# Activation halves moved 64 bytes apart in SBUF under a three-product float32r matmul kernel

## What is computed

```python
def conv_ffn(h, w_in, conv_w, conv_b, w_out):
    a = dwconv3(h @ w_in, conv_w, conv_b)
    gate, up = jnp.split(a, 2, axis=-1)
    return (jax.nn.silu(gate) * up) @ w_out
...
def _sq_relu_mlp(hn, w1, w2):
    a = jax.nn.relu(hn @ w1)
    return (a * a) @ w2
```

## Time and profile before

| | |
|---|---|
| time, median of 3 runs | 2044.6 us (2042.35 to 2045.34) |
| the profiled execution, its time | 2041.65 us |
| its span, first to last instruction | 2039.9 us |
| mean granted TensorE clock | 0.983 of full speed |
| TensorE matmul busy | 1938.5 us, 95% |
| weight load busy | 1709.0 us, 84% |
| DVE, ACT, POOL busy | 1251.0, 920.6, 217.7 us |

### The profile page before, as it was taken

The page is one execution under the profiler, slowest core; times in us unless marked ns, Lnnn a source line. Parts: engine busy times, 40 slices in busy tenths (PEclk is TensorE's granted clock), DMA queues, the critical chain, the costliest instruction groups (busy, mean ns, idle before and its releaser), DMA issues.

```text
span 2039.9 us, 33160 instructions
## 1 busy us (share of the span) xinstructions
PE 1938.5 (95%) x13225; PEld 1709.0 (84%) x13225; DVE 1251.0 (61%) x1853; ACT 920.6 (45%) x1438; POOL 217.7 (11%) x171
## 2 busy tenths in 40 slices
PE   4999989999999899999979998999999999989998
PEld 3776647778887479999979997998899999879997
DVE  6355466543654556678577767656975567787564
ACT  4344344322332242158465554347554444565353
POOL 2100104430542000011000000000010010000001
PEclk8999989999999899999999999999999999999999
DMA  8611464433222523223435544532444544224553
GB/s 357 229 69 63 164 228 165 167 125 111 83 90 85 206 83 128 101 83 104 145 136 170 208 162 142 174 137 83 139 171 167 177 174 145 94 94 170 186 182 124
DMA packets 43950, 296.78 MB, mean 145 GB/s; under 512 B 4976, under 2 KB 6128, under 8 KB 11696
## 3 DMA queue, kind: packets, MB, share of 16 engines
q1 hardware_dynamic: 36576, 247.48, 35.0%
q10 hardware_dynamic: 6048, 42.50, 5.9%
q0 software_dynamic: 1200, 5.02, 0.7%
HBM read 293.94 MB, written 1.05 MB: 145 GB/s over the span
## 4 chain that ended last, share of the span: by engine, by line
PE 83%; DVE 8%; ACT 4%; DMA 3%; issue 1%; POOL 1%; SPq 0%; ACTq 0%; DVEq 0%; POOLq 0%
PE acc L456 23%; PE acc L457 22%; PE acc L458 22%; DVE w_lo L393 2%; PE acc L451 2%; PE wk L550 2%; PE acc L453 2%; PE acc L452 2%; PE wk L1672 1%; DMA ada_first<-in_w_ada 1%; DMA ada_ring<-in_w_ada 1%; ACT w_hi L383 1%; PE wk L730 1%; PE acc L1661 1%; PE wk L1401 1%
## 5 line engine op out<-in xcount | busy, mean ns | idle before, releaser
L456 PE MATMUL acc<-Hhi,w_hi 128*128 128x272 f32 (+2 forms) x2304 | 740.5, 321 | 29.4 <-DVE Hlo L772 10.1
L457 PE MATMUL acc<-Hlo,w_hi 128*128 128x272 f32 (+2 forms) x2304 | 717.9, 312 | 0.0
L458 PE MATMUL acc<-Hhi,w_lo 128*128 128x272 f32 (+2 forms) x2304 | 717.5, 311 | 0.0
L393 DVE TENSOR_TENSOR w_lo<-w_raw,w_hi 128x1024 fp32r<-128x1024 f32 (+2 forms) x472 | 575.5, 1258 | 183.9 <-ACT w_hi L383 182.4
L383 ACT ACTIVATE w_hi<-w_raw 128x1024 fp32r<-128x1024 f32 (+2 forms) x472 | 452.3, 1005 | 432.9 <-PE acc L458 339.6
L456 PEld LDWEIGHTS acc<-Hhi,w_hi 128*128 128x128 f32 x2304 | 437.1, 190 | 79.7 <-issue 42.0
L457 PEld LDWEIGHTS acc<-Hlo,w_hi 128*128 128x128 f32 x2304 | 437.4, 190 | 22.1
L458 PEld LDWEIGHTS acc<-Hhi,w_lo 128*128 128x128 f32 x2304 | 436.5, 189 | 23.0
L456 PE MATMUL acc<-Fhi,w_hi 128*128 128x256 f32 (+2 forms) x864 | 265.1, 307 | 2.8 <-DVE w_lo L393 1.5
L458 PE MATMUL acc<-Fhi,w_lo 128*128 128x256 f32 (+2 forms) x864 | 264.6, 306 | 0.0
L457 PE MATMUL acc<-Flo,w_hi 128*128 128x256 f32 (+2 forms) x864 | 264.3, 306 | 0.0
(11 more groups left out here) (393 smaller groups left out, 2426.6 us busy)
## 6 DMA issues: line engine op xcount, KB each, us to landing
w_raw<-in_w_ffn_in SPq DMA_DIRECT2D x44, 1024.0 KB, 4.9
ada_ring<-in_w_ada ACTq DMA_DIRECT2D x40, 1024.0 KB, 4.9
w_raw<-in_w_mlp_in SPq DMA_DIRECT2D x32, 1024.0 KB, 4.9
w_raw<-in_w_mlp_out SPq DMA_DIRECT2D x32, 1024.0 KB, 4.9
w_raw<-in_w_ffn_out SPq DMA_DIRECT2D x32, 704.0 KB, 4.1
ada_first<-in_w_ada SPq DMA_DIRECT2D x8, 1024.0 KB, 18.4
w_raw<-in_w_ret_v SPq DMA_DIRECT2D x8, 1024.0 KB, 4.9
w_raw<-in_w_ret_g SPq DMA_DIRECT2D x8, 1024.0 KB, 4.8
```

Of the source, the lines that this page charges most:

```text
L393: dve.tensor_tensor(w_lo[:, r, a:b], w_raw[:, r, a:b], w_hi[:, r, a:b].bitcast(F32), ALU.subtract).then_inc(lo_done, 1)
L456: pe.matmul(o, w_hi[:, r, w], x_hi(k), start=k == 0, stop=False)
L457: pe.matmul(o, w_hi[:, r, w], x_lo(k), start=False, stop=False)
L458: mm = pe.matmul(o, w_lo[:, r, w], x_hi(k), start=False, stop=k == last)
```

## The change

The program keeps every instruction and their order on every engine; operands move. `A` goes from 64 to 128 modulo 256 (64 bytes further). The pairs, in bytes modulo 256, high half and low half:

| pair | before | after |
|---|---|---|
| H 512 (hyb, ffn0_in) | 192, 192 | 128, 192 |
| H 512 as read by ret_k, ret_q, ret_v, ret_g, now called R | 192, 192 | 192, 128 |
| H 256 (ffn1_in) | 192, 192 | 192, 128 |
| H 272 (ab, mlp0_in, c, mlp1_in) | 128, 128, then 64 more for each chunk | unchanged |
| F 512 (ffn0_out) | 64, 64 | 128, 192 |
| F 256 (ffn1_out) | 64, 64 | 192, 128 |
| F 272 (mlp0_out, mlp1_out) | 64, 64, then 64 more for each chunk | 128, 192; rows of 288 columns, then 128 more for each chunk |
| AT and SG (hyb_out) | 64, 64 | 128, 128 |
| rv_out (ret_out) | 64, 64 | 192, 192 |
| AB (ab_out0) | 64, 64, then 64 more for each chunk | 128, 128, then 64 more |

The remaining edits move work buffers by 64 bytes so that nothing overlaps. The diff, cut to its core:

```diff
-        A = (at_const[0] + 127) // 128 * 128 + 64
-
-        H_hi = {T1: at("Hhi512", [P, DC, T1], h0 + 64, F32R), SEQ: at("Hhi256", [P, 16, SEQ], h0 + 64, F32R),
+        A = (at_const[0] + 255) // 256 * 256
+
+        H_hi = {T1: at("Hhi512", [P, DC, T1], h0, F32R), SEQ: at("Hhi256", [P, DC, SEQ], h0 + 64, F32R),
                 T2: at("Hhi272", [P, 16, T2], h0, F32R)}
-        H_lo = {T1: at("Hlo512", [P, DC, T1], h0 + HB + 64, F32R), SEQ: at("Hlo256", [P, 16, SEQ], h0 + HB + 64, F32R),
+        H_lo = {T1: at("Hlo512", [P, DC, T1], h0 + HB + 256 + 64, F32R), SEQ: at("Hlo256", [P, DC, SEQ], h0 + HB + 256 + 0, F32R),
                 T2: at("Hlo272", [P, 16, T2], h0 + HB, F32R)}
+
+        R_hi, R_lo = at("Rhi", [P, DC, T1], h0 + 64, F32R), at("Rlo", [P, DC, T1], h0 + HB + 256 + 0, F32R)
...
-        F_hi = {T1: at("Fhi512", [P, FFH, T1], A + 16 * KB, F32R), SEQ: at("Fhi256", [P, FFH, SEQ], A + 16 * KB, F32R),
-                T2: at("Fhi272", [P, MLH, T2], A + 16 * KB, F32R)}
-        F_lo = {T1: at("Flo512", [P, FFH, T1], A + 38 * KB, F32R), SEQ: at("Flo256", [P, FFH, SEQ], A + 38 * KB, F32R),
-                T2: at("Flo272", [P, MLH, T2], A + 38 * KB, F32R)}
+        F_hi = {T1: at("Fhi512", [P, FFH, T1], A + 16 * KB, F32R), SEQ: at("Fhi256", [P, FFH, SEQ], A + 16 * KB + 64, F32R),
+                T2: at("Fhi272", [P, MLH, 288], A + 16 * KB + 0, F32R)}
+        F_lo = {T1: at("Flo512", [P, FFH, T1], A + 38 * KB + 64, F32R), SEQ: at("Flo256", [P, FFH, SEQ], A + 38 * KB + 0, F32R),
+                T2: at("Flo272", [P, MLH, 288], A + 38 * KB + 64, F32R)}
...
-        rv_out = at("rv_out", [P, 4, 2048], A + 16 * KB, F32R)
+        rv_out = at("rv_out", [P, 4, 2048], A + 16 * KB + 64, F32R)
...
-            ret = (lambda k: H_hi[T1][:, k, LAT:T1], lambda k: H_lo[T1][:, k, LAT:T1])
-            project(pe, "ret_k", *hyb, need=h_need(pe, 2))
+            both = (lambda k: R_hi[:, k, :], lambda k: R_lo[:, k, :])
+            ret = (lambda k: R_hi[:, k, LAT:T1], lambda k: R_lo[:, k, LAT:T1])
+            project(pe, "ret_k", *both, need=h_need(pe, 2))
```

More of the change, by code:

```diff
@@ L231, in stack_kernel @@
         ada_ring = at("ada_ring", [P, 2, SLOT], nt0 + 18 * KB)
-        ada_rows = [at("ada_rows0", [P, 2, 256], A + 32 * KB), at("ada_rows1", [P, 1, 256], h0 + 16 * KB + 64)]
+        ada_rows = [at("ada_rows0", [P, 2, 256], A + 32 * KB), at("ada_rows1", [P, 1, 256], h0 + 16 * KB + 128)]
         sq2 = at("sq2", [P, 2, T2], A + 85 * KB)
@@ L239, in stack_kernel @@
         last = at("last", [P, DC, SEQ], h0)
-        F_hi = {T1: at("Fhi512", [P, FFH, T1], A + 16 * KB, F32R), SEQ: at("Fhi256", [P, FFH, SEQ], A + 16 * KB, F32R),
-                T2: at("Fhi272", [P, MLH, T2], A + 16 * KB, F32R)}
-        F_lo = {T1: at("Flo512", [P, FFH, T1], A + 38 * KB, F32R), SEQ: at("Flo256", [P, FFH, SEQ], A + 38 * KB, F32R),
-                T2: at("Flo272", [P, MLH, T2], A + 38 * KB, F32R)}
[L245 to L248, removed]
+        F_hi = {T1: at("Fhi512", [P, FFH, T1], A + 16 * KB, F32R), SEQ: at("Fhi256", [P, FFH, SEQ], A + 16 * KB + 64, F32R),
+                T2: at("Fhi272", [P, MLH, 288], A + 16 * KB + 0, F32R)}
+        F_lo = {T1: at("Flo512", [P, FFH, T1], A + 38 * KB + 64, F32R), SEQ: at("Flo256", [P, FFH, SEQ], A + 38 * KB + 0, F32R),
+                T2: at("Flo272", [P, MLH, 288], A + 38 * KB + 64, F32R)}
+        cgu = at("cgu", [P, 2, 2, T1], A + 60 * KB + 64)
+        sg = at("sg", [P, 2, T1], A + 68 * KB + 64)
+        hid = at("hid", [P, 2, T1], A + 72 * KB + 64)
+        hid2 = at("hid2", [P, 2, 2, T2], A + 72 * KB + 64)
         g_sb = at("g_sb", [P, 4, T1], A + 16 * KB)
@@ L266, in stack_kernel @@
         ro = at("ro", [P, 8, 2, SEQ], A)
-        rv = at("rv", [P, 4, 2048], A + 16 * KB)
-        rv_out = at("rv_out", [P, 4, 2048], A + 16 * KB, F32R)
[L269 to L277, removed]
+        rv = at("rv", [P, 4, 2048], A + 16 * KB + 64)
+        rv_out = at("rv_out", [P, 4, 2048], A + 16 * KB + 64, F32R)
+        r_ctx = at("r_ctx", [P, 2, SEQ], A + 88 * KB + 64)
+        rq = at("rq", [P, 8, SEQ], A + 48 * KB + 64)
+        rg = at("rg", [P, 16, SEQ], A + 56 * KB + 64)
+        r_dist = at("r_dist", [P, 2, 2, SEQ], A + 72 * KB + 64)
+        r_dec = [at(f"r_dec{i}", [P, 4, SEQ], A + (76 + 4 * i) * KB + 64) for i in range(2)]
+        r_rope = at("r_rope", [P, 2, 2, SEQ], A + 80 * KB + 64)
+        r_e = at("r_e", [P, 2, SEQ], A + 84 * KB + 64)
+        r_rs = at("r_rs", [P, 2, SEQ], A + 86 * KB + 64)
+        r_sq = at("r_sq", [P, 2, SEQ], A + 90 * KB + 64)
         qk = at("qk", [P, 16, T2], A)
@@ L759, in act_norm @@
                 act.wait_ge(n32_ready, DC * j + c + 1)
-                act.activation(H_hi[n][:, c, 0:n], n32[:, c % 2, 0:n], ACT.Copy).then_inc(hhi_ready, 1)
+                hi = R_hi if j == 2 else H_hi[n]
+                act.activation(hi[:, c, 0:n], n32[:, c % 2, 0:n], ACT.Copy).then_inc(hhi_ready, 1)
         def dve_norm(dve, j, meanwhile=None):
@@ L771, in lo @@
                 dve.wait_ge(hhi_ready, DC * j + c + 1)
-                dve.tensor_tensor(H_lo[n][:, c, 0:n], n32[:, c % 2, 0:n], H_hi[n][:, c, 0:n].bitcast(F32),
+                hi, lo = (R_hi, R_lo) if j == 2 else (H_hi[n], H_lo[n])
+                dve.tensor_tensor(lo[:, c, 0:n], n32[:, c % 2, 0:n], hi[:, c, 0:n].bitcast(F32),
                                   ALU.subtract).then_inc(h_ready, 1)
@@ L3002, in _ @@
             pe_ada_close(pe, ADA_RING)
-            ret = (lambda k: H_hi[T1][:, k, LAT:T1], lambda k: H_lo[T1][:, k, LAT:T1])
-            project(pe, "ret_k", *hyb, need=h_need(pe, 2))
+            both = (lambda k: R_hi[:, k, :], lambda k: R_lo[:, k, :])
+            ret = (lambda k: R_hi[:, k, LAT:T1], lambda k: R_lo[:, k, LAT:T1])
+            project(pe, "ret_k", *both, need=h_need(pe, 2))
             pe.wait_ge(s_mod, 9)
             project(pe, "ret_q", *ret)
-            project(pe, "ret_v", *hyb, after=lambda s: (all_freed(pe, "ret_q") if s == 0 else None,
+            project(pe, "ret_v", *both, after=lambda s: (all_freed(pe, "ret_q") if s == 0 else None,
                                                         pe_rope(pe, rope_items(), [2 * s, 2 * s + 1], SEQ, swap_ret, 0)))
```

## The result

The changed kernel takes 2053.0 us (median of 6 runs, 2051.22 to 2055.59) against 2043.13 us for the kernel before (median of 6 in the same comparison): ratio 1.0051, 95% interval 1.0039 to 1.0062. It is slower by 10 us, where I forecast 24 us less.

A forecast was written before the change was run, and what follows sets the result against it. TensorE's pace per triple was taken to bound the kernel; one-step gains of 9.6 us (512 columns), 7.6 (ret_g, ffn1_in, ffn1_out1), 3.8 (mlp1_out) and 3.4 (mlp0_out) summed to 24.4 us, giving 2020 us, range 2003 to 2050.

The forecast's parts named there:

- What bounds the kernel, and that pace goes into the span one to one: Whole kernel: TensorE matmuls in flight 95% of the span, so time is triples times pace, passing nearly one to one.
- All 544 triples of H 512 at 686.8 ns: All 512-column stages up to ret_k: 544 triples counted at 686.8 ns, the pace read in ffn0_in1.
- Placement can set the pace: TensorE operand streams: addresses are one thing that can set the pattern behind each triple's 20 to 60 ns surplus.
- every touched triple that isn't already at the fastest pace seen for its width gains one step: Touched `project` stages: the likeliest case, 24.4 us less in sum, chance 0.42.
- one step: Pace of a triple: the 13.4 ns between ffn1_out0 and ffn1_out1, taken as the gain per touched triple.
- a zero in the sum: ret_v and hyb_v, 320 "tok" triples with activations loaded: at most 4.3 us either way, taken as zero.
- 340 against 353 ns: 256-column stages: ffn1_out0 and ret_q at 340.0 ns a triple, ffn1_out1 and ffn1_in1 at 353.4.
- 11.4 (the 256-column stages and mlp1_out): Gains of 7.6 us for ret_g, ffn1_in and ffn1_out1, and 3.8 us for mlp1_out.
- Terms taken as zero: AT and SG (at most 0.9 us either way), rv_out, and hyb_v with ret_v (at most 4.3 us): all zero.
- The slower rival: Touched triples: a moving operand jumping 64 bytes costs time itself, together 13.8 us more, 2058 us; chance 0.15.
- Cover: ffn1_in1: one step makes 56 us 53.9, DVE at 85% and still hidden; its `w_lo` would be late next.

The follow-up runs named there:

- before_again: The kernel before, unchanged, profiled a second time: 2043.13 us, ratio 1.0004 (0.9994 to 1.0014).
- w192_in192: in192 with w_hi and w_lo also moved 64 bytes, to 192 modulo 256: 2048.73 us, 1.0034 against the kernel before.
- in192: Changed kernel's layout with both halves of every pair except H 272 in step at 192 modulo 256: 2038.72 us, 0.9979 against the kernel before.
- in64: Changed kernel's layout with both halves of every pair except H 272 in step at 64 modulo 256: 2045.37 us, 1.0016 against the kernel before.
- in0: Changed kernel's layout with both halves of every pair except H 272 in step at 0 modulo 256: 2054.7 us, 1.0059 against the kernel before.
- wlo192_in128: Changed kernel's layout with pairs except H 272 in step at 128, w_hi at 128, w_lo moved to 192: 2048.44 us, 1.0027 against the kernel before.

## Why the prediction was wrong

- *What bounds the kernel, and that pace goes into the span one to one*: right. From the first triple of a stage to the first of the next, the changed kernel against the second profile of before has hyb_out 1.0 us less, the four ffn0 stages 2.0 more (the last without the stretch behind it), ret_k, ret_q and ret_v 4.2 more, ret_g and ret_out 0.5, the four ffn1 stages 2.2: together 7.9 us. The stretch between ffn0_out1 and ret_k has 2.45 us more and all the rest 0.4 less, which makes the 10.0 us between the two profiled executions. The 2.45 us are no matter of pace, and 1.8 of them also separate the two profiles of before; whether the placement has a part in them stays open.
- *All 544 triples of H 512 at 686.8 ns*: wrong for 96 of them. The triples of hyb_qk0 to hyb_qk3 and hyb_u start some 790 ns apart in both kernels, and from hyb_g to hyb_out it took 169.33 us in before_again and 169.29 in the changed kernel. At 13.4 ns each they put 1.3 us into the sum that no pace could give.
- *Placement can set the pace*: right. In step, four places give 680 to 700 ns with the same instructions. As to the rule of the Trainium skill (TensorE: Matmul & The Clock Gate, Part 2) that the moving operand and the weight load read through independent ports: w192_in192 and in192 differ, as far as places modulo 256 go, by the place of the weights alone, and with 512 columns their paces differ by 7 ns. The measurement decides: where the weights stand does affect the pace at which the moving operand streams.
- *"every touched triple that isn't already at the fastest pace seen for its width gains one step"*: this step failed, in sign. I had no row for halves out of step, took as its price one step, the difference between two patterns at one placement with 256 columns and between two placements with 512, and gave it the sign of a gain. Out of step by 64 bytes costs with 512 columns: F 512 696 instead of the 682 of its places. With 256 columns it brings the dearer place for the low half and takes the fast pattern away: 357 ns, where the same stages had 340 or 353. ret_v, a zero in the sum, lost as much as any. That 353.4 - 340.0 and 700.0 - 686.8 came out as the same 13 ns was luck: the first is a pattern that varies with the execution, the second is a difference between two places, 64 and 192, which the in-step runs repeat at will.
- *340 against 353 ns*: read as something that placement could secure. before_again shows that it varies with the execution at one placement. Of the forecast's 24.4 us, 11.4 (the 256-column stages and mlp1_out) rested on it.
- *Terms taken as zero*: hyb_out became 1.0 us shorter, about the 0.9 us that I gave as its bound. ret_v, where the activations are the loaded operand, took 2.8 us more than in the first profile of before and 3.2 more than in the second, inside the 4.3 for it and hyb_v. The bounds were good and the second zero was not.
- *The slower rival* named a mechanism that fits with 512 columns, a jump of 64 bytes, and its bill was 13.8 us against the measured 9.9: H 512 7.2 where the paces give at most 5.1 with ret_k, since most of it stopped at 696; ret_v 3.4 where it is 2.8 to 3.2; ret_q and the fast half of ffn1_out 2.3, which depends on the patterns of the execution. What it left out are the gains of F 512 and hyb_out, 1.5 us, because their place before was the worst of four. Its evidence was weak all the same: mlp1_out at 355 ns, which I took for the price of a jump of 64 bytes, takes 353 in in192, 350 in in64 and 357 in in0, all without such a jump.
- *Cover*: DVE's `w_lo` never came to the front, as the earlier trace rows had it; L458 waits 1.5 us for it in ffn1_out, as before.

What stays open: why a jump of 64 bytes costs with 512 columns, little or nothing with 256 where the activations stream, and helps with 272 in one direction; what share of it comes from the weights' side (wlo192_in128 fits neither reading), so that JUMP is a name for the cost and not a shown mechanism; and what throws a stretch of 256 columns into one pattern or the other at a pause.

## What to carry to other kernels

Where TensorE is the bound and streams float32r operands, the place of an operand in SBUF modulo 256 bytes against that of the weights is worth up to 3% of a matmul's pace, in either direction, and its best value depends on the number of columns; measure all four places in step before trying two at once. Read a pace over some 25 triples, on both sides of a pause, in several stages and in two executions before calling a difference of a few per cent an effect: two stretches, or two runs, with the same addresses can differ by 4%. When paces are added up to explain a difference in time, add up the stretches between them too; here one of them differed by 1.8 us between two executions of one kernel. When the trace holds no case of what a change does, the difference between two existing patterns gives a size at most and never a sign.

## What the runs showed of the hardware that I had not expected

- With float32r and 512 moving columns a triple takes 680, 687, 697 or 700 ns as the moving operand begins 0, 64, 128 or 192 bytes after the weights' place modulo 256; with 256 columns 360, 353, 356 or 353 in ffn1_in1, and also 340 in other stretches at 64 and 192.
- The place is relative: weights and activations moved together by 64 bytes give the same paces (680 and 360 ns) as neither moved.
- With 512 columns, halves 64 bytes apart: 696 ns where the places average 682, and 693 or 700 in the other direction where they average 685; 128 bytes apart: 691 ns where they average 691.
- A stretch of 256 columns in step at distance 64 or 192 runs at 340 or at 353 ns a triple, and changes from one to the other only at a pause of the stream.
- In the changed kernel's ffn1_in1 the second matmul of every other chunk is the slow one. Its starts in the timeline:

```profile
1155.18 0.29 PE L459 MATMUL acc<-Hlo,w_hi 128*128 128x256 f32 x1
...
1155.54 0.28 PE L459 MATMUL acc<-Hlo,w_hi 128*128 128x256 f32 x1
1155.66 0.28 PE L460 MATMUL acc<-Hhi,w_lo 128*128 128x256 f32 x1
```

The next matmul after the first of these starts at 1155.31 (shown above), 0.13 us later, the one after the second 0.12 us later. In the ns of the trace it is 127 or 128 for every other chunk, and 116 to 118 for every other matmul of the stage.
